# Where the three stages of the split weights lie in SBUF, against the turned tokens

## The reference, cut to what matters

```python
proj = einsum('bsd,de->bse', rmsnorm(h, mix_norm_pre[layer]), w_in[layer])      # 1024 -> 2048
u, q, k, v = the four quarters of proj
mix = einsum('bse,ed->bsd', concat([pool_mixer(u), attention(q, k, v)]), w_out[layer])
h = h + rmsnorm(mix, mix_norm_post[layer])
hn = rmsnorm(h, ffn_norm_pre[layer])
f = (silu(hn @ wg) * (hn @ wu)) @ wd          # layer 0: dense, 1024 -> 4096 -> 1024
f = moe_swiglu(hn, ...)                       # layer 1: 8 experts, 1024 -> 3584 -> 1024, 2 per token
h = h + rmsnorm(f, ffn_norm_post[layer])
```

## The kernel before, in words

| tensor | address | mod 512 |
|---|---|---|
| ring, three buffers of 16384 bytes | 38080 | 192 |
| w_hi, three stages of 8192 | 87232 | 192 |
| w_lo, three stages of 8192 | 111808 | 192 |
| uT, pt23, h, gpost, win_b, router_sb, rows, cols | from 136384 to 163872 | |
| spare (filler up to the end of the expert slots) | 163872 | |
| hs | 176256 | 128 |
| hT_hi (ypT_hi lies over it) | 184448 | 128 |
| hT_lo (yaT_hi, and yaT_lo 4096 further, lie over it) | 192640 | 128 |
| dhid_hi, over qT | 24704 | 128 |
| dhid_lo, over kT | 28800 | 128 |
| ypT_lo | 218496 | 384 |

## Time and profile before

### The profile page before, as it was taken

How to read it: one execution, slowest core, us unless ns; L and a number is a source line. 1 busy time by engine, 2 the same in 40 slices (tenths; PEclk the granted TensorE clock), 3 DMA queues, 4 the chain that set the end, 5 groups by cost and what they waited for, 6 DMA issues and landing times.

```text
span 1312.7 us, 31092 instructions
## 1 busy us (share of the span) xinstructions
PE 1284.1 (98%) x14401; PEld 792.6 (60%) x14401; DVE 414.2 (32%) x581; ACT 277.9 (21%) x430; POOL 108.0 (8%) x240
## 2 busy tenths in 40 slices
PE   8999999999999999999999999999999999999996
PEld 8888999999989863354353364345353354346333
DVE  6886555555576950030210120030030031031011
ACT  4665344444464630000000000000000000000101
POOL 4134300000000307300000000000000000000000
PEclk9999999999999999999999999999999999999998
DMA  9547855555544399999999999999999999999994
GB/s 304 218 154 222 265 193 193 193 193 192 193 151 148 110 425 426 427 423 414 426 426 424 425 425 427 426 423 425 426 424 425 425 426 424 426 425 425 425 424 167
DMA packets 66868, 443.50 MB, mean 338 GB/s; under 512 B 4504, under 2 KB 10656, under 8 KB 42160
## 3 DMA queue, kind: packets, MB, share of 16 engines
q1 hardware_dynamic: 64592, 433.58, 81.2%
q0 software_dynamic: 2144, 7.90, 2.1%
HBM read 439.36 MB, written 2.10 MB: 336 GB/s over the span
## 4 chain that ended last, share of the span: by engine, by line
PE 89%; DMA 4%; DVE 3%; SPq 2%; ACT 1%; issue 1%; ACTq 0%; DVEq 0%
PE psum L1060 38%; PE psum L1069 18%; PE psum L718 9%; PE psum L720 9%; PE psum L719 9%; DMA unit<-in_moe_w_down 3%; PE psum L1004 2%; PE psum L1015 1%; DMA ring<-in_w_in 1%; PE psum L808 1%; SPq L376 1%; PE psum L739 1%; PE psum L798 1%; ACT pt L1209 1%; DVE hs L1495 0%
## 5 line engine op out<-in xcount | busy, mean ns | idle before, releaser
L1060 PE MATMUL psum<-unit,xT 128*32 128x448 f32 x5376 | 507.0, 539 | 0.1
L1060 PEld LDWEIGHTS psum<-unit,xT 128*32 128x32 f32 x5376 | 174.4, 110 | 327.4 <-issue 325.2
L1069 PE MATMUL psum<-unit,hid 128*32 128x256 f32 x4704 | 259.3, 379 | 3.8 <-DMA unit<-in_moe_w_down 3.8
L1069 PEld LDWEIGHTS psum<-unit,hid 128*32 128x32 f32 x4704 | 151.4, 110 | 109.1 <-DMA unit<-in_moe_w_down 5.7
L1725 DVE TENSOR_TENSOR hidp<-hid,psum 128x448 f32<-128x448 f32 x42 | 38.4, 914 | 535.4 <-PE psum L1060 535.4
L1401 DVE TENSOR_TENSOR w_lo<-ring,w_hi 128x2048 fp32r<-128x2048 f32 x64 | 148.3, 2323 | 120.2 <-ACT w_hi L1172 119.9
L718 PE MATMUL psum<-hT_hi,w_hi 128*128 128x256 f32 x656 | 183.0, 279 | 0.4 <-DVE qT L1521 0.3
L720 PE MATMUL psum<-hT_hi,w_lo 128*128 128x256 f32 x656 | 181.8, 277 | 0.0
L719 PE MATMUL psum<-hT_lo,w_hi 128*128 128x256 f32 x656 | 181.8, 277 | 0.0
L1172 ACT ACTIVATE w_hi<-ring 128x2048 fp32r<-128x2048 f32 x72 | 137.4, 1912 | 64.8 <-PE psum L720 52.5
L718 PEld LDWEIGHTS psum<-hT_hi,w_hi 128*128 128x128 f32 x656 | 123.3, 188 | 2.4 <-issue 1.4
(11 more groups left out here) (251 smaller groups left out, 943.3 us busy)
## 6 DMA issues: line engine op xcount, KB each, us to landing
unit<-in_moe_w_gate SPq DMA_DIRECT2D x64, 1792.0 KB, 33.2
unit<-in_moe_w_up SPq DMA_DIRECT2D x64, 1792.0 KB, 27.6
unit<-in_moe_w_down SPq DMA_DIRECT2D x64, 1792.0 KB, 32.8
ring<-in_dense_w_gate SPq DMA_DIRECT2D x8, 2048.0 KB, 9.0
ring<-in_dense_w_up SPq DMA_DIRECT2D x8, 2048.0 KB, 9.0
ring<-in_dense_w_down SPq DMA_DIRECT2D x8, 2048.0 KB, 8.3
ring<-in_w_in SPq DMA_DIRECT2D x6, 2048.0 KB, 8.8
ring<-in_w_out SPq DMA_DIRECT2D x4, 2048.0 KB, 8.6
```

Of the source, the lines that this page charges most:

```text
L1060: ins = mm(bank(half, s)[quad(j)], xT[:, s, dt, :], w[:, at:at + FJ], start=dt == 0, stop=dt == DT - 1)
L1069: ins = mm(down_out[s][quad(j)], e[:, half, s, t, :], w, start=half == t == 0 and s != 2, stop=half == 1 and t == FT - 1, skip_group_check ...
```

## The change

`w_hi` and `w_lo` are no longer one tensor of three stages each but three tensors each. In front of each a filler is put, so that it begins at a chosen remainder modulo 1024. With HT_AT = 128, the remainder of the turned tokens, the stages of `w_hi` begin at 128 + 64, 128 + 128 and 128 + 192, those of `w_lo` at 128 + 576, 128 + 640 and 128 + 704. Modulo 512 these are 64, 128 and 192 bytes from the tokens. Everything that reads or writes a stage takes the tensor of that number in place of the slice. No instruction is added, removed or moved in its engine's order, and no semaphore or wait is changed.

```diff
-        w_hi = sb("w_hi", [P, STAGE, 8 * C2], F32R)
-        w_lo = sb("w_lo", [P, STAGE, 8 * C2], F32R)
+        HT_AT = 128
+
+        def staged(name, apart):
+
+            out_ = []
+            for k, n in enumerate(apart):
+                gap = (HT_AT + n - plan_top[0]) % 1024
+                if gap:
+                    sb(f"{name}_gap{k}", [P, gap // 4])
+                out_.append(sb(f"{name}{k}", [P, 8 * C2], F32R))
+            return out_
+
+        w_hi = staged("w_hi", (64, 128, 192))
+        w_lo = staged("w_lo", (576, 640, 704))
...
-        assert plan_top[0] <= nc.sbuf_usable_end
+        assert plan_top[0] <= nc.sbuf_usable_end and addr["hT_hi"] % 1024 == addr["hT_lo"] % 1024 == HT_AT
...
-                hi, lo = w_hi[:, n % STAGE, :], w_lo[:, n % STAGE, :]
+                hi, lo = w_hi[n % STAGE][:, :], w_lo[n % STAGE][:, :]
...
-                return w_hi[:, n % STAGE, :], w_lo[:, n % STAGE, :]
+                return w_hi[n % STAGE][:, :], w_lo[n % STAGE][:, :]
...
-                w = [a.rearrange("p (t n) -> p t n", t=DT) for a in (w_hi[:, half % STAGE, :], w_lo[:, half % STAGE, :])]
+                w = [a.rearrange("p (t n) -> p t n", t=DT) for a in (w_hi[half % STAGE][:, :], w_lo[half % STAGE][:, :])]
```

## The result

| | before | after |
|---|---|---|
| median, 6 runs each, us | 1314.67 | 1320.17 |
| lowest to highest | 1313.34 to 1316.1 | 1319.33 to 1320.82 |
| profiled execution, its span | 1314.47, 1312.7 | 1319.33, 1317.4 |

The ratio is 1.004, with a 95% interval from 1.003 to 1.005. The changed kernel is 5.5 us slower; the two profiled executions are 4.9 us apart.

The account below looks back on a forecast made before the run. TensorE was taken to bound the dense part and mixings, with the expert weight stream setting the end. Terms 0 + 0 + 0.4 + 0 + 0 = +0.4 us on 1314.47 gave 1314.9, against the median 1315.0; range 1308.0 to 1320.5 us.

Parts of the forecast that it names:

- the likeliest case: Whole kernel: the two pitch levels stay, 1315.0 us, own range 1312.3 to 1317.3, chance 0.45.
- The bound and the way out: TensorE bounds the dense part; time lost before about 455 us delays the expert weight stream and reaches the end nearly whole.
- The fillers: Fillers of 64, 64, 384, 64 and 64 bytes ahead of the stage tensors only shift addresses; no instruction added, 0 us.
- the 1024 bytes: Low parts move another 512 bytes against the high ones; nothing new to TensorE, whose pieces already meet both remainders modulo 1024.
- the splits: VectorE's computing of w_lo from ring and w_hi, median 2292 ns: 0 us, ends +1.0 and -1.0 us.
- the tensors behind: uT to cols move by 640 bytes, 128 modulo 512; their readers are short pieces on other engines: 0 us.
- The pitch: Time between TensorE matmul starts, 113.4 or 118.1 ns at 256 columns: direct effect 0, ends 6.9 us more, 13.3 us less.
- The sum: All terms added over the whole kernel: 0 + 0 + 0.4 + 0 + 0 = +0.4 us.
- The slower rival: Dense part and both mixings: stages 1 and 2 locked on the long pitch, price 6.9 us, 1321.5 us, chance 0.28.
- Stage 0: Stage 0 lies 64 bytes from the tokens modulo 512 before and after, so the layout does nothing new there.
- Which of the two pitches is drawn anew: Each half meets another distance: 2.9 us less if all go short, 2.9 more if long ones double; taken +0.4 us.
- The formula of "Back-to-back issue gap": TensorE matmul spacing N/2.4 + 2.5 ns, 109.2 ns at 256 columns and 215.8 at 512; the trace did not agree.

## Why the prediction was right or wrong

The time lay in the range (1308.0 to 1320.5), 0.3 us below its upper end, but the likeliest case, 1315.0 us with no effect, did not come. The rival that did come is the slower one, 1321.5 us, which had a chance of 0.28 and lay outside the range itself. That the time is inside is luck: the price of that rival was put too high, and by more than the 1.0 us at which the range cut it off.

- *The bound and the way out* were right: TensorE in the dense part, and a loss there arrives at the end: +4.83 us at the first expert load, +4.80 at the last.
- *The fillers, the 1024 bytes, the splits, the tensors behind* at 0 were right: all at 64 gives 1.0001, and one low part at 192, which moves the tensors behind by 128 bytes, 0.9983 and 1.0. VectorE's median split went from 2292 ns to 2293.
- *The pitch* is the step that failed: "Three distances, then, and the same two levels. I take 0 for the direct effect." The levels were nearly the same, but which distance can hold the lower one was not asked for all three operands together, and no row had 128. The three distances in the rows were 64, 64 the other way (448) and, for one load in three and 512 columns, 192. The runs bear out what they say: 448 can be short (the kernel before has such a piece itself, 113.2 ns from 408.07 to 410.56 us), and even with 256 columns a low part at 192 is free. But a low part at 128 costs the whole 4.8 ns, and in the down product 0.08 us a block. The sum put 0.4 us; the dense part alone measured 4.68.
- *The slower rival* had the mechanism in its effect (a long pitch in stages 1 and 2), and its price was too high: 6.9 us worked out, 5.5 measured between the medians and 4.8 between the profiles. Of the 6.9 us, 4.8 are in the dense part by its own shares (819 x 4.64 + 224 x 4.3 ns), and 4.68 were measured there. The other 2.1 are in the two mixings, where TensorE grew by 1.4 us and the path by 0.15 (0.46 less up to the dense part, 0.61 more up to the first expert load). So what was mis-sized is the mixings: in the first of them above all TensorE waits for other things (it is busy 105.89 of 112.50 us), and the price was added as if it did not. The counts differ little: by the stages 1584 and 360 matmuls moved, not 1536 and 384. Why its pitch is long, the next weights' read meeting the running stream, no run shows.
- Stage 0, where it was, won back a little, as the halves before it no longer keep it long: the first five halves behind the opening take 28.14 us instead of 28.34 (from 118.20 to 146.34 us in the changed kernel's timeline).
- *Which of the two pitches is drawn anew:* its spread, 2.9 us either way, was too small: at 64 all of the dense part can be long, 1319.85 us in one profiled run.
- *The splits:* their bound in the dense part was worked out with 32 halves; there are 48. Nothing hangs on it, as the median split stayed.
- The rule of the Trainium skill weighed there ("TensorE: Matmul & The Clock Gate", section "Step-by-step: what each phase is for") is that reading the next weights out of SBUF takes nothing from the running matmul. By it the distance would not matter, and these fp32r matmuls do not agree: all at 64 they can be 113.3 ns apart, all at 128 they are 118.6 to 120.0. The measurement decides; that the two meet at SBUF is not shown by it.
- The formula of "Back-to-back issue gap" weighed beside it is, by that section of the Trainium skill, for a matmul by itself; for a stream of weight loads and matmuls the section gives about 131 ns at 512 columns, and the 227.5 to 234.2 ns here agree with that still less.

## What to carry to other kernels

Where a kernel is bound by matmuls with a weight load each, compare the distance of two matmul starts with the columns at the clock; a few ns of excess in thousands of matmuls can hang on where the two operands start, modulo 512 bytes. Give each buffer of a rotation another distance once and read the pitch by buffer from one profile. Then run all buffers at the best distances, each alone, since a pitch also depends on what ran before. And before a tuned layout is disturbed, see whether it is on a good place by chance: here the tensors stood at a distance at which most of the dense part is on the short pitch, and nothing in the code said so.

## What the runs showed of the hardware that was not expected

- With stationary pieces of 512 bytes and moving rows of 1024 bytes in fp32r, the pitch depends on the distance between the two modulo 512. In the dense part it was 113.3 ns at 64 and 116.7 to 120.0 at eleven others; in pieces of the mixings it was 113.3 at 320 and 448 too, and never at 0, 32, 96, 128, 160, 224, 256 or 384. With 512 moving columns it is 227.5 ns at 256, 229.0 at 64, 233.3 at 448, 234.2 at 160.
- The pitch has a memory. At 64 it is 113.3 or 117.8 ns, at 128 it is 118.5 or 120.0, and each holds for up to hundreds of matmuls; with high parts at 192 and low ones at 64 a half takes 5.44 or 5.70 us by what ran before it.
- One load of three at 128 makes all three matmuls long (118.1 ns in the mean); one of three at 192 does not (113.3 to 114.1 in the dense part).
- Why this is so is open. The pitches of 113.3 and 229 ns are themselves above 106.7 and 213.3 ns, which 256 and 512 columns would take at one per clock of 2.4 GHz (an estimate, as in the prediction's sum), and no distance tried removed that.
